# Two transformer blocks on one core: seven weight splits put ahead of norm steps, copies and stores

## What is computed

```python
def first_block(x, ...):
    n = rms_norm(h, norm_mix_pre)
    z_gmlp, q, k, v, gates = split(n @ w_in)
    y_a = gmlp_spatial_gating(gelu(z_gmlp), ...)
    y_b = mix of three dilated window attentions over q, k, v
    g_a, g_b = split(sigmoid(gates + b_gate))
    merged = g_a * (y_a @ w_branch_a) + g_b * (y_b @ w_branch_b)
    h = h + rms_norm(merged @ w_out, norm_mix_post)
    n2 = rms_norm(h, norm_mlp_pre)
    h = h + rms_norm(square(relu(n2 @ w_up)) @ w_down, norm_mlp_post)
    return h
```

## Time and profile before

| | us |
|---|---|
| median of 3 runs | 2115.59 (2115.19 to 2117.29) |
| the profiled execution | 2114.54 |
| its span (first to last instruction) | 2112.6 |
| mean granted TensorE clock | 0.995 |
| PE busy | 2058.2 (97%) |
| DVE busy / ACT busy | 945.7 (45%) / 844.6 (40%) |

### The profile page before, as it was taken

The page is one execution under the profiler, slowest core; times in us unless marked ns, Lnnn a source line. Parts: engine busy times, 40 slices in busy tenths (PEclk is TensorE's granted clock), DMA queues, the critical chain, the costliest instruction groups (busy, mean ns, idle before and its releaser), DMA issues.

```text
span 2112.6 us, 26911 instructions
## 1 busy us (share of the span) xinstructions
PE 2058.2 (97%) x11129; PEld 1765.9 (84%) x11129; DVE 945.7 (45%) x1329; ACT 844.6 (40%) x1173; POOL 17.3 (1%) x36
## 2 busy tenths in 40 slices
PE   7999999999999999989999999999999999999999
PEld 7889888789888888887889888888877789888887
DVE  4744453324543344556663433433543345433343
ACT  4332233323533332557763333333455435333332
POOL 1000000000000000010000000000000000000000
PEclk9999999999999999999999999999999999999999
DMA  7222221232222333211102223333222212332232
GB/s 226 71 70 80 70 70 60 80 110 90 90 91 98 99 99 99 73 45 42 41 21 80 95 86 99 99 99 99 81 75 65 80 61 81 100 99 85 94 100 82
DMA packets 169688, 178.98 MB, mean 85 GB/s; under 512 B 6769, under 2 KB 139454, under 8 KB 169346
## 3 DMA queue, kind: packets, MB, share of 16 engines
q1 hardware_dynamic: 168424, 176.58, 26.4%
q0 software_dynamic: 1024, 1.12, 0.2%
q10 hardware_dynamic: 154, 0.04, 0.0%
HBM read 174.50 MB, written 2.10 MB: 84 GB/s over the span
## 4 chain that ended last, share of the span: by engine, by line
PE 89%; DVE 5%; ACT 4%; issue 1%; DMA 0%; ACTq 0%; DVEq 0%
PE psum L82 27%; PE psum L84 27%; PE psum L83 27%; PE psum L1800 1%; DVE weights_lo L317 1%; PE psum L760 1%; PE psum L1778 1%; PE psum L738 1%; ACT weights_hi L311 1%; PE psum L2208 1%; PE psum L430 1%; PE psum L1788 1%; DVE weights_lo L1419 1%; PE psum L1756 0%; DVE norm_T_lo L450 0%
## 5 line engine op out<-in xcount | busy, mean ns | idle before, releaser
L82 PE MATMUL psum<-norm_T_hi,weights_hi 128*128 128x512 f32 (+1 forms) x1440 | 539.0, 374 | 7.0 <-DVE weights_lo L317 5.0
L84 PE MATMUL psum<-norm_T_hi,weights_lo 128*128 128x512 f32 (+1 forms) x1440 | 534.4, 371 | 0.0
L83 PE MATMUL psum<-norm_T_lo,weights_hi 128*128 128x512 f32 (+1 forms) x1440 | 534.0, 371 | 0.0
L82 PE MATMUL psum<-weights_hi,act_T_hi 128*128 128x512 f32 (+2 forms) x976 | 367.4, 376 | 11.1 <-DVE weights_lo L1419 3.3
L83 PE MATMUL psum<-weights_lo,act_T_hi 128*128 128x512 f32 (+2 forms) x976 | 364.4, 373 | 0.0
L84 PE MATMUL psum<-weights_hi,act_T_lo 128*128 128x512 f32 (+2 forms) x976 | 364.3, 373 | 0.0
L82 PEld LDWEIGHTS psum<-norm_T_hi,weights_hi 128*128 128x128 f32 x1440 | 271.8, 189 | 56.5 <-DVE weights_lo L317 5.9
L1323 ACT ACTIVATE weights_hi<-raw_weights 128x2048 fp32r<-128x2048 f32 x92 | 175.7, 1909 | 342.3 <-PE psum L84 342.3
L84 PEld LDWEIGHTS psum<-norm_T_hi,weights_lo 128*128 128x128 f32 x1440 | 271.6, 189 | 46.8
L83 PEld LDWEIGHTS psum<-norm_T_lo,weights_hi 128*128 128x128 f32 x1440 | 271.9, 189 | 45.5
L1419 DVE TENSOR_TENSOR weights_lo<-raw_weights,weights_hi 128x2048 fp32r<-128x2048 f32 x92 | 210.9, 2292 | 106.6 <-ACT weights_hi L1323 106.6
(11 more groups left out here) (252 smaller groups left out, 1929.7 us busy)
## 6 DMA issues: line engine op xcount, KB each, us to landing
raw_weights<-in_ffn_w_dram SPq DMA_DIRECT2D x64, 1024.0 KB, 5.2
raw_weights<-in_w_in_dram SPq DMA_DIRECT2D x36, 512.0 KB, 4.7
raw_weights<-in_w_up_dram SPq DMA_DIRECT2D x16, 1024.0 KB, 5.6
raw_weights<-in_w_down_dram SPq DMA_DIRECT2D x16, 1024.0 KB, 4.9
raw_weights<-in_w_in_dram SPq DMA_DIRECT2D x12, 1024.0 KB, 5.2
raw_weights<-in_mlstm_w_in_dram SPq DMA_DIRECT2D x8, 1024.0 KB, 5.0
raw_weights<-in_w_out_dram SPq DMA_DIRECT2D x4, 1024.0 KB, 5.1
raw_weights<-in_mla_w_o_dram SPq DMA_DIRECT2D x4, 1024.0 KB, 5.1
```

The lines of the kernel that those rows point to most:

```text
L82: pe.matmul(out, ah, bh, start=start, stop=False)
L83: pe.matmul(out, ah, bl, start=False, stop=False)
L84: return pe.matmul(out, al, bh, start=False, stop=stop)
```

## The change

Seven units of weights are split earlier in the order of ACT and DVE, one small activation is added, and at two places PE runs a product group before a set of transposes where it ran it after. No product, shape or buffer changes. The diff, cut to the lines and their neighbours:

```diff
@@ gmlp, ACT
                 act.wait_ge(cleared.sem, cleared.at(1))
+                act.activation(SM[:, 163:164], EPSC, ACT.Sqrt)
                 act.wait_ge(param.sem, param.at(16))
                 norm.pair_sum(act, 0)
                 split_hi(act, u0)
                 act.wait_ge(v1.sem, v1.at(1))
                 norm.hi(act, 0)
+                split_hi(act, u0 + 1)
                 act.wait_ge(x_ld.sem, x_ld.at(16))
                 norm.pair_sum(act, 1)
-                split_hi(act, u0 + 1)
                 norm.hi(act, 1)
@@ gmlp, DVE
                 norm.pair_sum_beside(dve, 1)
+                split_lo(dve, u0 + 1)
                 norm.normed(dve, 1)
-                split_lo(dve, u0 + 1)
                 norm.lo(dve, 1)
@@ dilated, ACT, after the last head's last step
+                split_hi(act, ug + 3)
                 store(NH - 1)
@@ dilated, DVE
+                split_lo(dve, ug + 3)
                 store(NH - 1)
@@ gates, ACT
                         early = j == 0 and q < 2
-                        if not early:
+                        if j or q == 3:
                             split_hi(act, u0 + 6 * j + q + 1)
...
                     act.activation(NTH[:, k, :], SG[:, k // 4, k % 4, :], ACT.Copy).then_inc(th.sem, 1)
+                    if k == KD - 2:
+                        split_hi(act, u0 + 13)
@@ gates, DVE
-                    for q in range(0 if j else 2, 5):
+                    for q in range(0 if j else 3, 5):
                         split_lo(dve, u0 + 6 * j + q + 1)
...
+                split_lo(dve, u0 + 13)
                 lo(7)
@@ out_product, ACT
                     nxt.hi(act, 0)
+                    split_hi(act, u0 + 5)
                     squared(1, 3)
                     rooted(3)
-                    split_hi(act, u0 + 5)
@@ out_product, DVE
                     nxt.lo(dve, 0)
+                    split_lo(dve, u0 + 5)
                     scaled(1, 3)
                     updated(1)
-                    split_lo(dve, u0 + 5)
@@ ffn, PE
                 up_half(1, 0, 0)
+                up_half(1, 1, 0)
                 if whole_in:
                     norm.turned(pe, 1)
-                up_half(1, 1, 0)
@@ ffn, ACT
                     rooted(2)
+                    split_hi(act, u0 + 4 * NF + 1)
                     squared(1, 3)
                     rooted(3)
-                    split_hi(act, u0 + 4 * NF + 1)
@@ ffn, DVE
                     landed(1, 2)
+                    split_lo(dve, u0 + 4 * NF + 1)
                     landed(1, 3)
                     updated(1)
-                    split_lo(dve, u0 + 4 * NF + 1)
@@ mla_down, PE
                 second(0)
+                second(1)
                 norm.turned(pe, 1)
-                second(1)
@@ build
-            came = out_product(block, "out1", ..., banks, norm, NTH, NTL, made, early, freed)
+            came = out_product(block, "out1", ..., banks, norm, NTH, NTL, made, early, freed, ahead=1)
```

More of the change, by code:

```diff
@@ L2480, in build @@
             early = [(j, range(NT), k, k + 4) for k in (0, 4) for j in (0, 1)]
-            came = out_product(block, "out1", A["norm_mix_post"][0:1, :], banks, norm, NTH, NTL, made, early, freed)
+            came = out_product(block, "out1", A["norm_mix_post"][0:1, :], banks, norm, NTH, NTL, made, early, freed, ahead=1)
             after = norm_halves(C_N0, *turn[1], halves, whole=True)
```

## The result

| | before | after |
|---|---|---|
| median of 4 runs, us | 2115.65 (2115.19 to 2117.29) | 2101.97 (2101.08 to 2106.86) |
| profiled execution / its span | 2114.54 / 2112.6 | 2101.08 / 2099.1 |
| mean granted TensorE clock | 0.995 | 0.997 |

The ratio is 0.9942, 95% interval 0.9930 to 0.9953. The forecast was 2101.0, in a range of 2096.5 to 2106.5. The total is 1 us off; its terms are not all right, and that is what the rest is about.

The account below looks back on a forecast made before the run. PE, 89% of the chain, was taken as the bound, with time lost in its waits and at lower clock. 2.0 + 5.0 + 1.5 + 0.7 + 5.4 = 14.6 us gave a median of 2101.0, range 2096.5 to 2106.5.

Parts of the forecast that it names:

- Place 1: Begin: table load moved into idle time, unit 0 split sooner, wait of 1.29 gone; 2.0 us, bounds 1.0 to 3.0.
- Place 2: Start of the gates: wait of 3.23 goes and the clock stays up, 3.4 plus 1.6; 5.0 us.
- place 3: End of the gates: unit out1+1 split after slice 6, so the wait of 1.48 goes; 1.5 us.
- place 4: Head of ffn1: wait of 1.54 goes, less 0.8 for the late norm of half 1; 0.7 us.
- Place 5: End of ffn1, head of mla_down: wait of 4.07 shrinks to 1.7; 5.4 us if the clock stays, about 4.8 of it clock.
- Rival A: The clock still falls at the head of mla_down, around the transposes: 2102.6 us, or 2105.8 if long; chance 0.17.
- Rival B: Half 1's norm path becomes the bound in ffn1 and mla_down, 1.9 lost twice: 2104.8 us; chance 0.11.
- Rival C: Clock falls elsewhere, as within 1116 to 1122.9, go too: 3.2 us, 2097.8; chance 0.06.
- D: Slower: the clock falls in mLSTM passages where it had held, 12 falls, 2120 us; chance 0.02.
- E: Units still wait for landing or buffer, so splits run at the old times: 2115 us; chance 0.02.

Follow-up runs that it names:

- only_place2: The kernel before with only the edit at the start of the gates (unit gates+3 split ahead of the stores); 2111.93 us, one run.
- no_place4: The changed kernel with the edit at the end of out1 and the head of ffn1 undone; 2104.46 us, one run.
- only_place5: The kernel before with only the edit at the end of ffn1 and the head of mla_down; median 2113.42 us, ratio 0.9998.
- fill_unit_wait: The changed kernel with 13 unread products of 256 columns in the wait of 1.69 for unit mla_down+1; 2097.17 us, one run.
- wide_second: The changed kernel with the products of unit mla_down+1 256 columns wide instead of 160; median 2101.79 us, ratio 0.9939 to the kernel before.
- split_sooner_again: The changed kernel with unit mla_down+1 split two steps sooner, run again on another chip; median 2101.49 us, ratio 0.9934 to the kernel before.
- old_pe_order: The changed kernel with PE's old order in ffn1 and mla_down, early splits kept; median 2109.06 us, ratio 0.9977 to the kernel before.
- split_sooner: The changed kernel with unit mla_down+1 split two steps sooner; median 2102.86 us, ratio 0.9943 to the kernel before.
- after_again: The changed kernel run once more, unedited; median 2104.78 us, ratio 0.9953 to the kernel before.
- sooner_filler_wide: The changed kernel with unit mla_down+1 split sooner, unread products in PE's waits and 256-column products of that unit; median 2103.11 us, ratio 0.9935.
- no_root_first: The changed kernel without the root on one column ahead of the wait for x; 2107.74 us, one run.

## Why the prediction was right, and where not

| term | forecast | measured | from |
|---|---|---|---|
| 1 begin | 2.0 | 2.6 | transposes of half 1 |
| 2 start of gates | 5.0 | 5.1 (5.2 alone) | milestone 0.79, only_place2 |
| 3 end of gates | 1.5 | 1.7 | no_place4 |
| 4 head of ffn1 | 0.7 | 0.8 | no_place4 |
| 5 head of `mla_down` | 5.4 | 1.9 (1.0 from only_place2's stretch) | milestones 0.71 and 0.85 |
| unedited | 0 | 1.4 | fall at 986 gone |
| sum | 14.6 | 13.5 | spans 2112.6, 2099.1 |

**Place 1** gave 2.6 in the profile of after and 2.8 from ACT's first use of x over all profiles, within the bounds of 1.0 to 3.0. The working gave 0.9 + 1.29 = 2.2 and cut it because more products would fall into the slow start; it was the other way round. The first product came at 15.04 and in the other new begins at 14.5 to 14.9, where 14.6 was forecast (15.56 before), so that term held. The miss is behind it: from the first product to half 1 it was 26.47 - 15.56 = 10.9, and is 23.86 - 15.04 = 8.8, so 2.1 where the 1.29 of the wait stood. The other 0.8 is the slow start: the first five products of before took over 0.39 us each, and none of after did.

**Place 2** held in both halves, the wait and the clock: with the wait of 3.23 gone the fall was gone too, in all twelve profiles that have the edit. The 1.6 for it was the price of a fall of 3.4 us; only_place5 shows that it could be 6.8.

**Places 3 and 4** held within 0.2; place 3 was never run alone, its 1.7 is the 2.5 of both less place 4. The slack of 0.4 on which place 4 rested was real, and about the size said: the scaling ended at 536.97, PE came at 537.16. The wait on low parts was 0.53 for the 0.4 forecast. Undone, place 4 gave 0.8 away; with PE's old order and the early split kept, 1.9, which is 1.1 worse than no edit. So the new order of PE is what makes the early split pay there.

**Place 5 is where the prediction failed**, at the words "if the clock stays". The wait left was 1.69 for the 1.7 forecast, so the idle time was right; but the clock fell behind it, at 890.3. The prediction read the fall of before as standing behind the wait of 4.07; in fact it began in it, at 901.0, with the wait ending at 901.53. For the wait of 1.7 that was left it forecast none, and rival A put one at the transposes only. The gain of 0.6 in idle time was put too low as well: at half clock PE is slow enough for the scaling and the low parts to be there before it asks, and neither the 0.8 nor the 0.4 arises. So the stretch still gained 1.9, and the fall cost 3.0 to 3.3, not the 4.8 that the prediction put on it. With the wait filled the drawn course came true to 0.3, counted from the 65.0 of before. Why a wait of 1.69 still lets the clock fall stays open; the runs show that it does, and that filling the wait or removing it does away with the long fall.

**Rival A** was, in what it says of the clock, the case that happened, at a chance of 0.17. Its mechanism was not: it put the fall at 904.6 to 907.7 of its own times, at the transposes; the fall began at 890.3, while the transposes began at 897.96. Sixteen transposes between waits of 0.76 and 0.53 (fill_unit_wait) and behind a wait of 1.68 and two groups of wide products (wide_second) left the clock at 1.00. Nor does the row at 1116 speak for the transposes as the prediction has it: the clock fell there at 1119.5 only, with products of 256 columns behind a wait of 1.50, and the four transposes of that stretch lie ahead of the wait. The rule of the Trainium skill, "TensorE: Matmul & The Clock Gate", Part 4: PE-mode transpose, that transposes don't keep the clock up, is so neither needed for this fall nor refuted by these runs; the short falls of split_sooner_again and old_pe_order, which began at their transposes behind waits of 1.90 and 3.44, would fit it.

**Rival B** had one half: the late norm is the next wait as soon as the unit is on time (1.87 in split_sooner, 2.67 in old_pe_order), but with the new order 0.53 was all that showed at place 4. **Rival C** happened in small: one fall fewer in MLA, 1.4 of its 3.2. But after_again had two falls there of 6.8 us each, so this is the execution's, not the change's. **D and E** did not happen: every split moved, and the falls in the two profiles of the changed kernel stand at places where before, only_place2 or only_place5 have one too. One place in mLSTM, near 1685, where PE waits 1.46, shows a fall of 3.4 us in split_sooner_again and sooner_filler_wide and in no other profile.

The total came out within 1.0 because 3.5 too much at place 5 stood against 0.6 at the begin, 0.4 at places 2 to 4 and 1.4 at the unedited place too little; the 1.4 was luck. Over all ten runs of the changed kernel, in both groups, the median is 2103.4: 10.9 us faster than the 23 runs of before beside them (2114.3), 2.4 slower than forecast, inside the range.

## What to carry to other kernels

A weight split costs the engine that makes it two microseconds wherever it stands; put it ahead of norm steps, copies and stores wherever the matrix engine asks for it first, and give the matrix engine other work to do while the late norm arrives, or the gain goes into the next wait (here 0.8 gained with it, 1.1 lost without). Shortening a wait is not the same as removing it: where a wait of 1.7 us was left, the clock fell as it had behind 4.1 us, and filling it with unread products brought 3.0 to 3.3 us in the one profile taken, more than the 1.9 that shortening it by 2.4 had. Read edits of a few microseconds off milestones on either side of them; whole runs of one kernel differ here by 5 to 8 us.

## What was not expected of the hardware

- A wait of 1.69 us was followed by 10.3 us at 1.2 GHz where products of 160 columns came behind it, but one of 1.54 us before 256-column products, and one of 1.68 before the same products widened to 256, were followed by none. The width alone does not explain it, since the wait of 1.50 at the end of MLA has 256-column products behind it and a fall in 13 of 14 profiles; what does is open, and wide_second was profiled once.
- At half clock PE was busy without a break (10.30 of 10.30), and the clock stayed low all the same. How long a fall lasted differed between kernels with the same products behind the same wait: 10.2 us in after, 13.7 in no_root_first.
- Falls in MLA, near 965 and near 1105, came and went between two profiles of one kernel: none and 3.4 us in one, 6.8 and 6.8 in the other. The waits there are the same in every profile: 1.44 or 1.45 near 965, with a fall of 6.8 us within 3 us of it in nine of fourteen, and 1.50 near 1105, with one in thirteen. Filling or removing them was not tried; a fall of 6.8 us in which PE is busy throughout costs 3.4 us (an estimate), as much as the fall in `mla_down`.
- A root on one column, placed in idle time, moved a load of 1.28 us off the path, and the sum of squares behind it needed no load of its own.
